# Prompt attention on TensorE in pairs of steps: transpositions, scores of two units, transpositions, values of two units

## What is computed

```python
def nsa_prompt(h, w_in, ...):                    # 512 prompt tokens, 16 query heads in 4 groups of 4
    q, rows_c, rows_s, rows_w, gates = nsa_project(h, pos, w_in)
    kc, vc = compress(rows_c, ...)               # 31 compressed keys and values
    o_c, p_c = cmp_attend(q, pos, kc, vc)        # softmax over the compressed keys
    idx = select_blocks(p_c, pos, S // SEL_BLK)  # top 16 of 8 blocks of 64: all of them
    o_s = sel_attend_blocked(q, pos, idx, rows_s, SEL_QBLK)
    o_w = window_attend_prompt(q, rows_w)        # window 512, so causal over everything
    return nsa_combine(gates, o_c, o_s, o_w, w_out), ...
```

## Time and profile before

| what | value |
|---|---|
| median of 3 runs (lowest, highest) | 1634.25 us (1633.77, 1636.83) |
| profiled execution, first to last instruction | 1633.6 us |
| around that span in the profiled execution | nothing that is timed; the runs' time is the same measure |
| prompt attention's steps in that span | from 903.9 to 1078.3 us |
| PE (TensorE) busy over the span | 1589.3 us, 97% |
| DVE (VectorE), ACT (ScalarE), POOL busy | 49%, 42%, 14% |

### The profile page before, as it was taken

The page is one execution under the profiler, slowest core; times in us unless marked ns, Lnnn a source line. Parts: engine busy times, 40 slices in busy tenths (PEclk is TensorE's granted clock), DMA queues, the critical chain, the costliest instruction groups (busy, mean ns, idle before and its releaser), DMA issues.

```text
span 1633.6 us, 31861 instructions
## 1 busy us (share of the span) xinstructions
PE 1589.3 (97%) x13307; PEld 1453.7 (89%) x13307; DVE 797.2 (49%) x1314; ACT 679.8 (42%) x1302; POOL 229.6 (14%) x574
## 2 busy tenths in 40 slices
PE   8999999999999999999999899999999999999998
PEld 7999988699999999998999666667989999999997
DVE  5755452556531555337334576743165552355523
ACT  3222134455532554324332566654355552354522
POOL 3000010300000000002013345432020000000001
PEclk9999999999999999999999999999999999999999
DMA  7222328122233232332334400034202323323231
GB/s 223 83 75 78 104 73 206 25 78 77 84 93 99 78 84 80 94 95 54 112 106 92 167 16 2 1 94 99 80 27 78 87 69 103 95 82 99 58 89 55
DMA packets 187417, 138.50 MB, mean 85 GB/s; under 512 B 11376, under 2 KB 178576, under 8 KB 187248
## 3 DMA queue, kind: packets, MB, share of 16 engines
q1 hardware_dynamic: 179424, 113.26, 24.4%
q0 software_dynamic: 7888, 23.79, 5.2%
HBM read 128.21 MB, written 13.01 MB: 86 GB/s over the span
## 4 chain that ended last, share of the span: by engine, by line
PE 89%; DVE 5%; ACT 2%; POOL 1%; issue 1%; DMA 1%; POOLq 0%; SPq 0%; DVEq 0%; ACTq 0%
PE gemm L990 42%; PE gemm L648 18%; PE gemm L659 9%; PE misc L623 6%; PE gemm L1132 2%; PE misc L1163 2%; PE misc L721 1%; PE gemm L707 1%; DVE y L1727 1%; PE misc L1283 1%; PE gemm L745 1%; PE misc L745 1%; PE gemm L677 1%; DVE wL L1693 1%; DMA xin<-in_x_prompt 1%
## 5 line engine op out<-in xcount | busy, mean ns | idle before, releaser
L1693 DVE TENSOR_TENSOR wL<-raw,wH 128x2048 fp32r<-128x2048 f32 (+2 forms) x107 | 222.1, 2076 | 222.8 <-ACT wH L1318 222.7
L990 PE MATMUL gemm<-hH,wH 128*128 128x272 f32 x1280 | 268.5, 291 | 0.1
L990 PE MATMUL gemm<-hH,wL 128*128 128x272 f32 x1280 | 264.8, 288 | 0.0
L990 PE MATMUL gemm<-hL,wH 128*128 128x272 f32 x1280 | 264.0, 288 | 0.0
L990 PEld LDWEIGHTS gemm<-hH,wH 128*128 128x128 f32 x1280 | 200.5, 188 | 6.2 <-issue 4.9
L1318 ACT ACTIVATE wH<-raw 128x2048 fp32r<-128x2048 f32 (+2 forms) x107 | 185.2, 1731 | 48.3 <-PE gemm L648 31.1
L990 PEld LDWEIGHTS gemm<-hL,wH 128*128 128x128 f32 x1280 | 201.0, 188 | 0.0
L990 PEld LDWEIGHTS gemm<-hH,wL 128*128 128x128 f32 x1280 | 200.0, 189 | 0.0
L1959 DVE SCALAR_TENSOR_TENSOR conv<-up,rows_t,conv 128x560 f32<-128x560 f32 x88 | 70.6, 802 | 209.2 <-ACT conv L1318 209.2
L1318 ACT ACTIVATE up<-gemm 128x32 f32<-128x32 f32 (+2 forms) x264 | 66.0, 324 | 176.0 <-PE gemm L990 153.7
L648 PE MATMUL gemm<-hH,wH 128*128 128x272 f32 (+1 forms) x624 | 133.0, 294 | 0.8 <-issue 0.5
(11 more groups left out here) (370 smaller groups left out, 2849.1 us busy)
## 6 DMA issues: line engine op xcount, KB each, us to landing
raw<-in_f_w_in SPq DMA_DIRECT2D x88, 512.0 KB, 5.0
raw<-in_f_w_out SPq DMA_DIRECT2D x32, 704.0 KB, 4.6
raw<-in_e_w_in SPq DMA_DIRECT2D x12, 1024.0 KB, 5.2
raw<-in_o_w_in SPq DMA_DIRECT2D x10, 1024.0 KB, 5.2
raw<-in_e_w_out SPq DMA_DIRECT2D x4, 1024.0 KB, 6.4
raw<-in_o_w_out SPq DMA_DIRECT2D x16, 256.0 KB, 6.4
pages<-in_cache_cmp POOLq DMA_DIRECT2D x10, 256.0 KB, 4.8
xin<-in_x_prompt SPq DMA_DIRECT2D x2, 1024.0 KB, 7.7
```

The source lines that it names most:

```text
L990: ins = pe.matmul(gemm[odd][:, n, 0:TH], w, x[:, k, n * TH:(n + 1) * TH], start=(k == 0 and part == 0), stop=(k == nk - 1 and part == 2))
L1693: order(dve.tensor_tensor(unit_view(wL, u), unit_view(raw, u), unit_view(wH, u).bitcast(F32), ALU.subtract), lo_ready)
```

## The change

TensorE's loop takes two steps at a time. For the pair of steps n and n+1 (n even) it now does: the transposition of unit n-4, the scores of unit n and unit n+1, the transposition of unit n-3, the values of unit n-5 and unit n-4. The dummy products and the `turn_in` calls of two steps also come together. The lists of the other four engines are as before, and so are all waits; only where they stand on TensorE differs.

```diff
-            for n in range(N_UNITS + LAG + 1):
-                if n < LAG:
-                    stay_busy(4, b5)
-                if LAG <= n < N_UNITS + LAG:
-                    turn_probs(n - LAG)
-                if n < N_UNITS:
-                    if n % 36 == 0:
-                        for sem_ in qk_ev:
-                            pe.wait_ge(sem_, 3 + 3 * (n // 36))
-                    scores(n)
-                if 1 <= n < 7:
-                    turn_in(5 + n)
-                if n > LAG:
-                    mix_values(n - LAG - 1)
+            for first in range(0, N_UNITS + LAG + 2, 2):
+                if first < LAG:
+                    stay_busy(8, b5)
+                if LAG <= first < N_UNITS + LAG:
+                    turn_probs(first - LAG)
+                for n in (first, first + 1):
+                    if n < N_UNITS:
+                        if n % 36 == 0:
+                            for sem_ in qk_ev:
+                                pe.wait_ge(sem_, 3 + 3 * (n // 36))
+                        scores(n)
+                for n in (first, first + 1):
+                    if 1 <= n < 7:
+                        turn_in(5 + n)
+                if LAG <= first + 1 < N_UNITS + LAG:
+                    turn_probs(first + 1 - LAG)
+                for n in (first, first + 1):
+                    if LAG < n <= N_UNITS + LAG:
+                        mix_values(n - LAG - 1)
```

## The result

The changed kernel took 1650.59 us (1649.07 to 1650.85, 4 runs), the kernel before, on the same chip, 1634.01: a ratio of 1.0096 with a 95% interval of 1.0081 to 1.0111. By the medians it is 16.6 us slower, 1.0%. The forecast was 1644.8 with a range from 1638 to 1651, so the time lies at the range's upper end and 5.8 us above the forecast.

The account below looks back on a forecast made before the run. TensorE was taken to bound the long units, the chain through DVE, ACT and POOL partly the short ones. Terms 0.8 + 1.1 + 2.0 + 1.0 + 4.2 + 1.4 = 10.5 us slower gave 1644.8 us, range 1638 to 1651.

Parts of the forecast that it names:

- The wait on the slot: VectorE's copy of odd unit k+1 needs the pT slot values k-1 read; wait 0.62 us per pair at 512 keys.
- The cycle at 512 keys: TensorE's pair of steps, values k-1 to values k+1 (k even): 6.46 us against 6.20 before, 0.26 slower.
- The mechanism I forecast: Copy's wait in all pairs and POOL's chain where keys fall: 1639 to 1649 us, chance 0.72.
- Same-shape blocks save nothing: Rival: neighbouring scores or values on TensorE save no fixed part, 6 us more: 1651 us, chance 0.09.
- The saved changes of shape: TensorE: four changes of tile shape per pair instead of six; 0.36 us per pair, 13.0 over 36 pairs.
- The compressed units: Their short mask and factor instructions in VectorE's list, priced at nothing; up to 0.5 us each, 3 us more.
- POOL's chain: Mask, reciprocal and POOL's scaling queue behind VectorE's held copy, 4.26 us; falling keys and stage's end cost 4.2 us.
- The start: Neighbouring `turn_in` calls share one PSUM bank, so the second waits for a copy: 1.4 us, at most 1.9.
- two falls of the clock: Clock rival: more idle time in first and fifth groups halves the clock, adding 1 to 3 us; chance 0.06.
- So the whole sum reaches the end: After the stage, TensorE's later work starts that much later, so the full 10.5 us shows in the time.
- The drains decide: Rival: copies in odd steps are not held, 13.0 us saved: 1621.2 us, chance 0.07.
- saving and wait cancel: Rival: engines see ends 0.1 us sooner, POOL's chain keeps slack, pairs come out even: 1632 to 1637, chance 0.06.

Follow-up runs that it names:

- experiment 1: Changed kernel with a third slot for the transposed probabilities from unit 14 on: 1635.69 us, ratio 1.0015 to the kernel before.
- experiment 2: Control: kernel before, in its old order, with the same third slot for the transposed probabilities: 1633.61 us, ratio 1.0006.
- experiment 7: Changed kernel with third slot, VectorE's reciprocal ahead of copy and mask, and first eight steps one at a time: 1626.76 us, ratio 0.9955.
- experiment 8: Control: kernel before, in its old order, with VectorE's reciprocal moved ahead of the copy: 1631.46 us, ratio 0.9983.
- experiment 6: Changed kernel with VectorE's reciprocal moved ahead of the copy and the mask, nothing else: 1644.08 us, ratio 1.0053 to the kernel before.
- experiment 9: Changed kernel with only the values in pairs, each unit's scores standing alone again: 1682.89 us, ratio 1.0305 to the kernel before.
- experiment 5: Changed kernel with only the scores in pairs, first unit's values ahead of the second transposition again: 1639.80 us, ratio 1.0036.

## Why the prediction was right, and where it was short

**The wait on the slot: right, and shown.** "The copy can start only when values k-1 are done": in the trace it is values (L1163) that release the copy, experiment 1 takes the wait away and gets 14.9 of 16.6 us back, and experiment 2 shows that it was not there before. The cycle at 512 keys was forecast at 6.46 and measured 6.51 us.

**The range: met with luck.** The mechanism I forecast had 1639 to 1649 as its own range, and 1650.59 lies above that. The whole range reached 1651 only because same-shape blocks might save nothing, and that is not what happened.

**The saved changes of shape: right in size for a pair.** 0.20 for two scores against 0.21, 0.14 for two values against 0.15 (1.90 in experiment 1, two apart 2.04), and the pair without its wait is 5.83 instead of 6.20, 0.37 against the forecast 0.36. I took the first of two scores to be 0.85 and the second 1.06; they are 0.96 each, nearly the same sum. The Trainium skill ("TensorEngine Tiling (Array Packing)", Key Properties) has it that a change of tiling mode drains TensorE. The trace agrees: a block of values follows another 0.10 us after the last record, as records within a block do, and transpositions follow values after 0.20. The same page of the Trainium skill (PSUM Bottleneck) warns that copies out of PSUM may bind after tiling has sped TensorE up; here it was their start, not their rate: VectorE was busy 115 of 176 us of the stage already before and waited idle for the values. Over all 36 pairs 10.2 us were saved and not 13 (experiments 7 and 8).

**The sum, by kinds of pairs.** The stage, from the first transposition to what follows the last values, took 167.2 us before and 182.5 after, 15.3 more; the forecast had 10.5. Starts of the transpositions in the two timelines give, for the pairs as the prediction counts them (us):

| pairs | number | forecast | measured |
|---|---|---|---|
| at the start | 2 | 1.4 | 2.9 |
| 128 keys | 8 | 0.8 | 2.0 |
| 256 keys | 8 | 1.1 | 2.0 |
| 384 keys | 10 | 2.0 | 2.8 |
| 512 keys | 4 | 1.0 | 1.2 |
| the keys fall, or no scores left | 4 | 4.2 | 4.5 |

**The compressed units: the term that was mis-sized.** I priced them at nothing and looked only at their short instructions. But a compressed unit's copy has 1024 columns whatever the keys. The changed kernel's second group, 256 keys, DVE and PE:

```profile
936.09 1.21 DVE L2086 COPY pT_rows<-misc 31x1024 f32<-31x1024 f32 x1 [1.52 <-PE misc L1163]
937.45 0.63 PE L623 MATMUL misc<-ident_sb,pr 128*128 128x128 f32 x4 [1.26 <-DVE pT_rows L2086]
```

In the same place TensorE waited 0.39 us before. The three pairs in which VectorE or ScalarE copies such a unit at 128 keys grew by 0.39 to 0.47 us each where I had 0.1, the two at 384 keys ahead of a group of 512 by 0.50 where I had 0.2: together 2.3 for 0.7. Between experiments 8 and 6, where POOL's waits are mostly out of both orders, the same five grew by 0.40 to 0.52. So this is not POOL's chain. That it is the copy is read from the trace; no experiment took it away.

**POOL's chain: right in two places, lucky in a third.** In the first pair where the keys fall the odd transposition waits for POOL; the pair took 6.43 us against 6.42 forecast, and 5.91 in experiment 6. So did the first pair without scores (6.42 against 6.42). The last one took 5.76 to its last values against 5.75. For the second pair where the keys fall I had POOL's chain too, at 5.66 us. It took 5.84, but for another cause. The changed kernel on PE:

```profile
1001.57 1.06 PE L623 MATMUL misc<-ident_sb,pr 128*128 128x128 f32 x8 [0.61 <-DVE pT_rows L2086]
1003.83 1.07 PE L623 MATMUL misc<-ident_sb,pr 128*128 128x128 f32 x8 [0.56 <-ACT pT_rows L1323]
1007.41 1.03 PE L623 MATMUL misc<-ident_sb,pr 128*31 128x128 f32 x8 [0.61 <-DVE pT_rows L2086]
```

TensorE waits for ScalarE's copy of the even unit, which two short scores don't cover, and in experiment 6 the pair is as long (5.85).

I did not work the chain out for short units. The second group of the changed kernel, DVE, POOL and PE:

```profile
941.08 0.69 DVE L2086 COPY pT_rows<-misc 128x512 f32<-128x512 f32 x1 [0.18 <-PE misc L1157]
941.92 0.63 PE L623 MATMUL misc<-ident_sb,pr 128*128 128x128 f32 x4 [0.37 <-DVE pT_rows L2086]
942.63 1.09 POOL L2342 TENSOR_SCALAR pr<-pr,rscale,gN 128x256 f32<-128x256 f32 x2 [1.83 <-DVE rscale L2065]
943.78 0.66 PE L623 MATMUL misc<-ident_sb,pr 128*128 128x128 f32 x4 [0.17 <-POOL pr L2342]
945.98 0.63 PE L623 MATMUL misc<-ident_sb,pr 128*128 128x128 f32 x4 [0.52 <-DVE pT_rows L2086]
```

From the start of the copy to the odd transposition 2.70 us, while TensorE's own blocks need 0.84 + 0.56 + 0.53 + 0.53 = 2.46. The pair takes 4.06, not 3.76 as forecast, and 3.82 in experiment 6. As a whole POOL's part is still near the forecast: 6.5 us by experiment 6 less 2.6 by its control, experiment 8, is 3.9, and the forecast had some 3 in it, the falls of the keys and the end of the loop.

**The start.** Forecast 1.4 us. In the two places where `turn_in` calls now stand side by side the second waited 0.79 and 0.78 us for the copy, near the 0.95 I had; the first place lies ahead of the stage. The profile's first group grew by 3.2, of which 2.4 are two falls of the clock at 915.1 and 922.0, 3.4 us each (by experiment 1's first group); from 915.1 to 925.4 TensorE was busy 9.44 of 10.30 us by records stretched to the slow clock. I had given this 1 to 3 us and a chance of 0.06; it happened in this profile together with the main mechanism and not instead of it. It is a small part of the 16 us: one of the four runs of the changed kernel had a mean granted clock of 0.995, as high as the kernel before in its profile (0.994), and still took 1649.07 us.

**"So the whole sum reaches the end": not quite.** 1.5 us of it were absorbed by the late transfer shown above, and the fall of the clock behind that (at 1117.2 in the kernel before) is missing after. This is read from two profiles and was not tried by an experiment.

**What is missing.** Of the 4.8 us between 10.5 and 15.3, 1.5 belong to the start and its falls of the clock, 1.6 to the pairs with a compressed unit, and the rest is spread over the other pairs. Outside the stage the differences are small and of both signs: 1.3 us before it, where the lists are the same, 2.4 between there and the first transposition of probabilities (a fall of the clock at 901.5, and the dummy products that now stand together ahead of the masks), 3.6 back behind the stage.

**The rivals.** "The drains decide" and "saving and wait cancel" fell: the saving is real and the wait is larger. "Same-shape blocks save nothing" gave the measured time by chance and is refuted by the rows; a time alone would not have told it from my forecast.

## What to carry to other kernels

Before blocks of one kind are put side by side, list for each buffer who frees it and where the freeing block now stands: here two slots were enough for steps one by one and one too few for steps in pairs. A wait on such a slot costs twice, once itself and once through everything queued behind it on the in-order engine, and the second part is largest where little work is left to cover it: where the keys fall and at the end of the loop. Look also for a block whose size does not follow the others, as the compressed unit's copy here. With the slot added, the reciprocal ahead of the copy and the first steps left single, the same order was 0.45% faster than the kernel before instead of 1% slower.

## What the runs showed of the hardware

- A change of tile shape shows at both ends of a block: scores of 512 keys took 1.06 us before between two other shapes and 0.96 with one neighbour of their own kind, whether that stood ahead or behind. By the slope from 128 to 512 keys (0.42 to 1.06 us) 0.85 of it goes with the keys.
- Ahead of the stage and in it, the clock fell to 1.2 GHz at 901.5, 915.1 and 922.0 us in the changed kernel's profile, 3.4 us each time; in experiment 9, whose TensorE was idle longest in the stage, for 10.2 us at a time. In the kernel before and in experiments 1, 2, 5, 7 and 8 it stayed whole through the stage.
- A weight load that waits is no measure of lost time. In experiments 1, 6 and 7 loads waited 24 to 30 us for POOL's causal units, while the products behind them were held 6 us or less.
